# Attention of eight heads as one unrolled chain, with a one-pass causal mask and another order of the query blocks

## The chip, the cores and the metric

The kernel runs on one core of a Trainium2 chip. The metric is the device time of one execution in microseconds, as the median of several runs. A core has TensorE (PE in the profile, matmuls; its weight loads are PEld), VectorE (DVE), ScalarE (ACT), GpSimd (POOL) and SyncE (SP, which issues most transfers here). Each engine works through its own instructions in program order, and they wait for one another on semaphores.

## The reference, cut to what matters

The whole computation is a first block (modulated RMS norm, a gated short convolution, an MLP with squared ReLU) and a second block of two layers (attention and pooling, a gated feed-forward with a causal convolution, a conformer convolution, a feed-forward again), all in float32 for 512 positions of 1024 channels. The change touches the attention alone: 8 heads of 64 channels, causal, with a bias that is the difference of cumulated log forget gates.

```
q = rms_norm(q, q_g); k = rms_norm(k, k_g)            # 512 positions, 8 heads, 64 channels
c = cumsum(log_sigmoid(f_logit))                      # per position and head
s = q @ k^T * 64**-0.5 + c[query] - c[key]
s = where(key <= query, s, -inf)
out = softmax(s) @ v
```

## The kernel before, in words

Weights stream from HBM in units of 256 columns (RAW); ScalarE rounds them to WH in fp32r, VectorE keeps the rest in WL, and TensorE makes each product as three fp32r matmuls (high by high, low by high, high by low; lines 1270 to 1272). The attention stands between the input product of the even layer and its output product, and is not split into high and low: its matmuls are full f32, and each of them shows as two instructions on TensorE.

Positions are cut into 4 query blocks of 128. Query block qb needs qb + 1 key blocks. QS and KS hold two heads (97 rows: 64 channels, and rows 64 and 96 with the decay and constants, so that the score matmul of line 1442 adds the decays). A score sits negated in PSUM, hence the minimum in place of a maximum.

For a block the work goes round the engines like this. TensorE: score matmul (line 1442), then a second matmul with the identity as weights that adds MASK, an upper triangle of 1e30, to the last 128 columns (line 1443). VectorE: minimum along each row (line 1089). ScalarE: exp with the minimum as bias and the row sum as a by-product into PR (line 638). TensorE: transposes of PR's blocks (line 1451). ScalarE: copy from PSUM to PT (line 645). TensorE: value product (line 1459), two instructions for each key block. VectorE: reciprocal of the row sum (line 1092), then the scaled output into OT (line 1097).

The software pipeline is written by hand. In step s TensorE issues the score of block s, the transposes of block s-2 and the values of block s-3; ScalarE the exp of s and the copy of s-2; VectorE the minimum of s, the reciprocal of s-2, the output of s-4. Scores have four PSUM banks, the transposes two, the outputs two; PR and PT are double. The steps run over 8 blocks, those of two heads, in a hardware loop over 4 pairs of heads. Each turn of the loop fills and drains the pipeline. At its top VectorE writes QS and KS of both heads from QK (lines 1081 and 1083), ScalarE copies the decay rows from CR (lines 630 and 631), and TensorE makes three matmuls without a use, keep_busy(3, 2), which the trace has at line 1289 as six instructions. Within a head the blocks come with 1, 2, 3, 4 key blocks.

Before the loop GpSimd has begun the window sums of the pooling half (lines 411 and 417). After the loop TensorE waits for the last OT, turns OT (line 1465), makes the pooling product, and the output product follows. SyncE has loaded the first output units before.

Of the kernel before, what the change touches and what calls it, by code (L numbers as in the profile page):

```python
# [27 lines left out]
P = 128  # L28
# [86 lines left out]
ROOT_LATE = (ST_X2, ST_F0, ST_F1)  # L115


def program(nc, i, out):
    ctx = ExitStack()
    with ctx:  # L120
# [52 lines left out]
        IDENT = at("IDENT", 204.75, [P, P])  # L173
        ONES = at("ONES", 205.25, [P, P])
        BD = at("BD", 205.75, [P, P])
        MASK = at("MASK", 206.25, [P, P])
# [202 lines left out]
        def _(pool):  # L379
            for m, v in ((IDENT, 0.0), (ONES, 1.0), (BD, 0.0), (MASK, 0.0)):  # L380
                pool.memset(m[:, :], v).then_inc(s_const0, 1)
            pool.memset(sc_(S_EPS), EPS).then_inc(s_const, 1)
            pool.wait_ge(s_const0, 4)
            pool.affine_select(out=IDENT[:, :], in_=IDENT[:, :], compare_op=ALU.not_equal, fill=1.0, base=0,
                               pattern=[[-1, P]], channel_multiplier=1).then_inc(s_const, 1)

            pool.affine_select(out=MASK[:, :], in_=MASK[:, :], compare_op=ALU.is_ge, fill=MASKED, base=0,
# [34 lines left out]
            pool.memset(MASK[:, :], -1.0 / P).then_inc(g_k, 1)  # L422
# [39 lines left out]
        def _(act):  # L462
# [163 lines left out]
            with act.Fori(0, HEADS // 2) as pair:  # L626
                for h in range(2):
                    act.wait_ge(e_cr, 32)
                    act.wait_ge(a_qk, pair * 4 + (2 * h + 2))
                    act.activation(QS[64:65, h:h + 1, :], CR[64:65, ds(pair * 2 + h, 1), :], ACT.Copy).then_inc(a_row, 1)  # L630
                    act.activation(KS[96:97, h:h + 1, :], CR[96:97, ds(pair * 2 + h, 1), :], ACT.Copy).then_inc(a_row, 1)
                for s in range(10):
                    if s < 8:
                        n = (s % 4 + 1) * P
                        act.wait_ge(a_min, pair * 8 + (s + 1))
                        if s >= 2:
                            act.wait_ge(a_t, pair * 8 + (s - 1))
                        act.activation(PR[:, s % 2, 0:n], PS_[:, S_BANKS[s % 4], 0:n], ACT.Exp, scale=-1.0,
                                       bias=sc_(S_MN + s), accum_out=sc_(S_RS + s)).then_inc(a_e, 1)
                    if s >= 2:  # L640
                        k, n = s - 2, ((s - 2) % 4 + 1) * P
                        act.wait_ge(a_t, pair * 8 + (k + 1))
                        if k >= 2:
                            act.wait_ge(a_o, pair * 8 + (k - 1))
                        act.activation(PT[:, k % 2, 0:n], PS_[:, 4 + k % 2, 0:n], ACT.Copy).then_inc(a_tc, 1)
# [92 lines left out]
            for n in range(DC):  # L738
# [9 lines left out]
                for k in range(TAPS_PE[n]):  # L748
                    act.activation(DG[:, j, k, :], IDENT[:, :], ACT.Copy,
                                   scale=col("dw_w0", 8 * (TAPS - TAPS_PE[n] + k) + n)).then_inc(g_d, 1)  # L750
# [50 lines left out]
        def _(dve):  # L801
# [275 lines left out]
            with dve.Fori(0, HEADS // 2) as pair:  # L1077
                for h in range(2):
                    lo, hi = h * DH, h * DH + DH

                    stt(QS[0:DH, h:h + 1, :], QK[lo:hi, ds(pair, 1), :], small[lo:hi, S_Q8:S_Q8 + 1],
                        SQT[lo:hi, ds(pair, 1), :], ALU.mult, ALU.mult).then_inc(a_qk, 1)
                    stt(KS[0:DH, h:h + 1, :], QK[lo:hi, ds(pair + 4, 1), :], col("k_g")[lo:hi, :],
                        SQT[lo:hi, ds(pair + 4, 1), :], ALU.mult, ALU.mult).then_inc(a_qk, 1)
                for s in range(12):
                    if s < 8:
                        n = (s % 4 + 1) * P
                        dve.wait_ge(a_s, pair * 8 + (s + 1))
                        dve.tensor_reduce(sc_(S_MN + s), PS_[:, S_BANKS[s % 4], 0:n], AX.X, ALU.min).then_inc(a_min, 1)
                    if 2 <= s < 10:  # L1090
                        dve.wait_ge(a_e, pair * 8 + (s - 1))
                        dve.reciprocal(sc_(S_RR + s - 2), sc_(S_RS + s - 2)).then_inc(a_rr, 1)
                    if s >= 4:
                        k = s - 4
                        dve.wait_ge(a_o, pair * 8 + (k + 1))
                        dve.wait_ge(a_rr, pair * 8 + (k + 1))
                        dve.tensor_scalar(OT[:, k % 4, ds(pair * P + k // 4 * DH, DH)], PS_[:, k % 2, 0:DH],
                                          sc_(S_RR + k), None, ALU.mult).then_inc(a_oe, 1)
# [156 lines left out]
        def _(pe):  # L1255
# [30 lines left out]
            def keep_busy(n, bank=7):  # L1286

                for _ in range(n):
                    pe.matmul(PS_[:, bank, :], IDENT[:, :], VCOL[:, 0:T], start=True, stop=True)
# [32 lines left out]
            for t in range(VT):  # L1322
                n = TILE_ROWS[t]
                if t == 1:
                    pe.wait_ge(s_vin, 16 * (7 + 4 + 2 + 8))
                if t >= 2:
                    pe.wait_ge(s_ve, t - 1)
                pe.transpose(PS_[:, 6 + t % 2, 0:n], VROW[0:n, t, :], IDENT[0:n, 0:n]).then_inc(s_vt, 1)
                if t == 0:
                    pe.wait_ge(s_xin, 16)  # L1330
                    for c in range(DC):
                        if c >= 4:
                            pe.wait_ge(s_xe, c - 3)
                        for b in range(TB):
                            tr = pe.transpose(PS_[:, c % 4, b * P:b * P + P], XROW[:, b, c * P:c * P + P], IDENT[:, :])
                        tr.then_inc(s_xt, 1)
                    mod_product(1)
                    channel_sum(ST_X0)
# [93 lines left out]
            with pe.Fori(0, HEADS // 2) as pair:  # L1432
                keep_busy(3, 2)
                for s in range(11):
                    if s < 8:
                        h, qb, n = s // 4, s % 4, (s % 4 + 1) * P
                        pe.wait_ge(a_qk, pair * 4 + (2 * h + 2))
                        pe.wait_ge(a_row, pair * 4 + (2 * h + 2))
                        if s >= 4:
                            pe.wait_ge(a_e, pair * 8 + (s - 3))  # L1440
                        bank = PS_[:, S_BANKS[s % 4], :]
                        pe.matmul(bank[:, 0:n], QS[:, h, qb * P:qb * P + P], KS[:, h, 0:n], start=True, stop=True)  # L1442
                        pe.matmul(bank[:, n - P:n], IDENT[:, :], MASK[:, :], start=False, stop=True,
                                  skip_group_check=True).then_inc(a_s, 1)
                    if 2 <= s < 10:
                        k = s - 2
                        pe.wait_ge(a_e, pair * 8 + (k + 1))
                        if k >= 2:
                            pe.wait_ge(a_tc, pair * 8 + (k - 1))
                        for b in range(k % 4 + 1):  # L1450
                            tr = pe.transpose(PS_[:, 4 + k % 2, b * P:b * P + P], PR[:, k % 2, b * P:b * P + P], IDENT[:, :])
                        tr.then_inc(a_t, 1)
                    if s >= 3:
                        k = s - 3
                        pe.wait_ge(a_tc, pair * 8 + (k + 1))
                        if k >= 2:
                            pe.wait_ge(a_oe, pair * 8 + (k - 1))
                        for b in range(k % 4 + 1):
                            mm = pe.matmul(PS_[:, k % 2, 0:DH], PT[:, k % 2, b * P:b * P + P],  # L1459
                                           V[:, b, ds(pair * P + k // 4 * DH, DH)], start=(b == 0), stop=(b == k % 4))  # L1460
                        mm.then_inc(a_o, 1)
            pe.wait_ge(a_oe, 32)
            for c in range(4):
                for b in range(TB):
                    pe.transpose(PS_[:, c, b * P:b * P + P], OT[:, b, c * P:c * P + P], IDENT[:, :]).then_inc(a_ot, 1)
# [24 lines left out]
            def turned(nth, n):  # L1490

                for half in range(2):
                    bank = TURN_BANKS[(nth + half) % 4]
                    for b in range(2):
                        for c in range(2):
                            tr = pe.transpose(PS_[:, bank, b * UW + c * P:b * UW + c * P + P],
                                              X[:, 2 * n + c, (2 * half + b) * P:(2 * half + b) * P + P], IDENT[:, :])
                    tr.then_inc(s_yt, 1)
# [34 lines left out]
            def taps(n):  # L1533
# [12 lines left out]
                if n >= 2:  # L1546
                    mm = pe.matmul(o, MASK[:, :], CV[:, 0, :], start=False, stop=True)
# [21 lines left out]
            for n in range(DC):  # L1569
                unit_with_taps(n)  # L1570
                if n == 2:
                    pe.wait_ge(g_x, 1)
                    pe.matmul(PS_[:, TAP_BANKS[0][0], :], MASK[:, :], CV[:, 0, :], start=True, stop=True
# [64 lines left out]
```

## Time and profile before

| | |
|---|---|
| median of 3 runs | 1844.48 us (1842.78 to 2548.79) |
| profiled execution, own time | 1842.85 us |
| its span | 1841.1 us |
| busy PE / PEld / DVE / ACT / POOL | 95% / 76% / 59% / 38% / 7% |
| mean granted TensorE clock | 0.977 |
| moved by DMA | 176.14 MB, mean 96 GB/s |

The busy share of PE is that of overlapping instructions, so a start-to-start distance says more than a duration. The page also gives the chain of waits: followed back from the last instruction, at each step the thing that released it. A microsecond of work that is on that chain is a microsecond of the kernel; idle time elsewhere costs nothing.

### The profile page before, as it was taken

What the parts mean: (1) busy time and instruction counts of PE and PEld (TensorE: products, weight loads), DVE (VectorE), ACT (ScalarE), POOL (GpSimd) and SP (SyncE); (2) the same over time, 40 slices, a digit from 0 to 9 for tenths busy, and PEclk for the clock granted to TensorE, in tenths of its full rate; (3) what the DMA queues carried; (4) which work ended last, traced back from release to release, by engine and by line L of the source; (5) the groups of instructions that cost most, each with busy time, mean ns of one, the idle gap of its engine ahead of it and who ended that gap; (6) DMA issues with size and microseconds to landing.
All of it is one profiled execution on the core that took longest, in us unless ns stands there. A gap on an engine that the chain in (4) does not pass through costs nothing.

```text
span 1841.1 us, 21801 instructions
## 1 busy us (share of the span) xinstructions
PE 1754.4 (95%) x7714; PEld 1404.7 (76%) x7714; DVE 1081.0 (59%) x1647; ACT 692.5 (38%) x1000; POOL 132.3 (7%) x131
## 2 busy tenths in 40 slices
PE   4899999999999879989999999999998999999998
PEld 4788857888888658666888888877664788888887
DVE  5698846343434543545566474567998667366374
ACT  2222225231314232454443242344665454244242
POOL 0000000000000000300000000000896000000000
PEclk7799999999999989999999999999999999999999
DMA  7577412223333203200322223223221222323222
GB/s 237 161 228 229 138 46 91 92 92 94 107 96 108 69 23 115 70 1 3 106 97 92 91 91 114 91 69 92 69 69 46 69 92 91 109 81 107 91 80 80
DMA packets 182188, 176.14 MB, mean 96 GB/s; under 512 B 3160, under 2 KB 181596, under 8 KB 182124
## 3 DMA queue, kind: packets, MB, share of 16 engines
q1 hardware_dynamic: 182124, 175.29, 29.8%
q8 instruction: 39, 0.64, 0.2%
q14 instruction: 25, 0.20, 0.0%
HBM read 173.15 MB, written 2.10 MB: 95 GB/s over the span
## 4 chain that ended last, share of the span: by engine, by line
PE 89%; DVE 5%; issue 2%; ACT 2%; DMA 1%; DVEq 0%; SPq 0%; ACTq 0%
PE PSUM L1270 24%; PE PSUM L1272 24%; PE PSUM L1271 24%; PE PSUM L1544 2%; PE PSUM L1563 1%; PE PSUM L1565 1%; PE PSUM L1564 1%; PE PSUM L1315 1%; PE PSUM L1442 1%; PE PSUM L1459 1%; DMA XROW<-in_x 1%; DMA ARAW<-in_ada_w 1%; DVE SQ L821 1%; PE PSUM L1300 1%; PE PSUM L1356 0%
## 5 line engine op out<-in xcount | busy, mean ns | idle before, releaser
L472 ACT ACTIVATE WH<-RAW 128x1024 fp32r<-128x1024 f32 x280 | 287.1, 1052 | 766.9 <-PE PSUM L1272 749.4
L1270 PE MATMUL PSUM<-XH,WH 128*128 128x512 f32 x1232 | 483.1, 392 | 11.8 <-issue 10.8
L1271 PE MATMUL PSUM<-XL,WH 128*128 128x512 f32 x1232 | 480.3, 390 | 0.0
L1272 PE MATMUL PSUM<-XH,WL 128*128 128x512 f32 x1232 | 480.2, 390 | 0.0
L808 DVE TENSOR_TENSOR WL<-RAW,WH 128x1024 fp32r<-128x1024 f32 x280 | 342.3, 1246 | 10.0 <-ACT WH L472 9.4
L1270 PE MATMUL PSUM<-HH,WH 128*128 128x512 f32 x756 | 296.7, 393 | 8.1 <-DVE HL L1151 4.9
L1271 PE MATMUL PSUM<-HL,WH 128*128 128x512 f32 x756 | 295.5, 391 | 0.0
L1272 PE MATMUL PSUM<-HH,WL 128*128 128x512 f32 x756 | 295.2, 390 | 0.0
L1270 PEld LDWEIGHTS PSUM<-XH,WH 128*128 128x128 f32 x1232 | 231.9, 188 | 64.2 <-issue 15.6
L1271 PEld LDWEIGHTS PSUM<-XL,WH 128*128 128x128 f32 x1232 | 232.0, 188 | 49.0 <-issue 1.2
L1272 PEld LDWEIGHTS PSUM<-XH,WL 128*128 128x128 f32 x1232 | 231.8, 188 | 48.6
L1270 PEld LDWEIGHTS PSUM<-HH,WH 128*128 128x128 f32 x756 | 142.6, 189 | 41.1 <-DVE WL L808 5.7
L1272 PEld LDWEIGHTS PSUM<-HH,WL 128*128 128x128 f32 x756 | 142.6, 189 | 30.0
L1271 PEld LDWEIGHTS PSUM<-HL,WH 128*128 128x128 f32 x756 | 142.7, 189 | 29.5
L1127 DVE TENSOR_TENSOR ZP<-PSUM,R 128x512 f32<-128x512 f32 x88 | 56.7, 686 | 176.8 <-PE PSUM L1272 176.8
L891 DVE TENSOR_TENSOR X<-PSUM,X 128x512 f32 (+1 forms) x62 | 39.9, 685 | 158.5 <-PE PSUM L1272 152.4
L431 POOL TENSOR_TENSOR CP<-CP,PRD 128x512 f32<-128x512 f32 x68 | 93.0, 1367 | 458.8 <-ACT PRD L763 450.2
L1138 DVE SCALAR_TENSOR_TENSOR TA<-ZP,VCOL,TA 128x512 f32<-128x512 f32 x176 | 120.1, 743 | 0.0
L1203 DVE SCALAR_TENSOR_TENSOR PSUM<-UPAD,VCOL,PSUM 128x512 f32<-128x512 f32 x121 | 81.8, 747 | 0.4
L836 DVE SCALAR_TENSOR_TENSOR MACC<-ARAW,small,MACC 128x256 f32<-128x256 f32 x140 | 67.9, 485 | 5.0
L1004 DVE TENSOR_SCALAR TA<-PSUM 128x512 f32<-128x512 f32 x32 | 20.6, 685 | 84.9 <-PE PSUM L1272 84.9
L685 ACT ACTIVATE TA<-ZP,VCOL 128x512 f32<-128x512 f32 x88 | 66.7, 805 | 0.0
(237 smaller groups left out, 1671.5 us busy)
## 6 DMA issues: line engine op xcount, KB each, us to landing
RAW<-in_ffn_w_up SPq DMA_DIRECT2D x44, 1024.0 KB, 5.1
ARAW<-in_ada_w SPq DMA_DIRECT2D x24, 1024.0 KB, 5.3
RAW<-in_mlp_w_in SPq DMA_DIRECT2D x16, 1024.0 KB, 5.3
RAW<-in_mlp_w_out SPq DMA_DIRECT2D x16, 1024.0 KB, 4.9
RAW<-in_ffn_w_down SPq DMA_DIRECT2D x16, 1024.0 KB, 5.1
RAW<-in_sc_w_in SPq DMA_DIRECT2D x12, 1024.0 KB, 5.1
RAW<-in_even_w_in SPq DMA_DIRECT2D x8, 1024.0 KB, 5.4
RAW<-in_odd_w_pw SPq DMA_DIRECT2D x16, 512.0 KB, 4.7
```

The source lines that it names most:

```text
L431: pool.tensor_tensor(CP[:, n, :], CP[:, n, :], PRD[:, before % RING, :], ALU.add).then_inc(g_a, 1)
L472: act.activation(WH[:, j, a:b, :], RAW[:, j, a:b, :], ACT.Copy).then_inc(s_hi, 1)
L685: act.activation(TA[:, c, :], ZP[:, c, 2:T + 2], ACT.Identity, scale=col(f"fw{layer}2", it * 2 + (half + 2 * first + c)), bias=col(f"fb{la ...
L808: tt(WL[:, j, a:b, :], RAW[:, j, a:b, :], WH[:, j, a:b, :].bitcast(F32), ALU.subtract).then_inc(s_lo, 1)
L836: stt(dst, w, s, dst, ALU.mult, ALU.add).then_inc(s_as if k < 7 else s_ad, 1)
L891: ins = dve.tensor_copy(d, src) if first else tt(d, src, d, ALU.add)
L1127: tt(ZP[:, c, 2:T + 2], banks(j, c), R[:, :], ALU.mult).then_inc(f_z, 1)
L1138: stt(TA[:, c, :], ZP[:, c, tap:tap + T], col(f"fw{layer}{tap}", it * 2 + (half + 2 * first + c)), TA[:, c, :], ALU.mult, ALU.add).then_in ...
L1203: stt(acc, src, w, acc, ALU.mult, ALU.add).then_inc(g_v, 1)
L1270: pe.matmul(o, wh, mh[:, k, :], start=(k == 0), stop=False)
L1271: pe.matmul(o, wh, ml[:, k, :], start=False, stop=False)
L1272: mm = pe.matmul(o, wl, mh[:, k, :], start=False, stop=(k == kn - 1))
```

## The change

There is no loop over pairs any more. All 32 blocks form one chain of steps (TensorE 35, ScalarE 34, VectorE 36), written out. Head n uses half n % 2 of QS and KS. Heads 0 and 1 are prepared ahead of the chain; heads 2 to 7 inside it: VectorE's scaled_head(n) stands behind the step of the first block of head n-1, ScalarE's decay_rows(n) behind the step of its second block. keep_busy(3, 2) runs once. IDENT and MASK are declared in fp32r, so that the mask matmul is one instruction; all other uses read them as f32. The blocks of a head are taken in the order of QUERY_BLOCKS, with 4, 1, 3 and 2 key blocks.

```diff
+QUERY_BLOCKS = (3, 0, 2, 1)
-        IDENT = at("IDENT", 204.75, [P, P])
+        IDENT = at("IDENT", 204.75, [P, P], F32R)
-        MASK = at("MASK", 206.25, [P, P])
+        MASK = at("MASK", 206.25, [P, P], F32R)
...
-            with act.Fori(0, HEADS // 2) as pair:
...
+            def decay_rows(n):
+
+                act.wait_ge(e_cr, 32)
+                act.wait_ge(a_qk, 2 * n + 2)
+                act.activation(QS[64:65, n % 2, :], CR[64:65, n, :], ACT.Copy).then_inc(a_row, 1)
+                act.activation(KS[96:97, n % 2, :], CR[96:97, n, :], ACT.Copy).then_inc(a_row, 1)
+
+            decay_rows(0)
+            decay_rows(1)
+            for s in range(4 * HEADS + 2):
+                if s < 4 * HEADS:
+                    n = (QUERY_BLOCKS[s % 4] + 1) * P
+                    act.wait_ge(a_min, s + 1)
                     if s >= 2:
+                        act.wait_ge(a_t, s - 1)
+                    act.activation(PR[:, s % 2, 0:n], PS_[:, S_BANKS[s % 4], 0:n], ACT.Exp, scale=-1.0,
+                                   bias=sc_(S_MN + s % 8), accum_out=sc_(S_RS + s % 8)).then_inc(a_e, 1)
+                if s >= 2:
+                    k, n = s - 2, (QUERY_BLOCKS[(s - 2) % 4] + 1) * P
+                    act.wait_ge(a_t, k + 1)
+                    if k >= 2:
+                        act.wait_ge(a_o, k - 1)
+                    act.activation(PT[:, k % 2, 0:n], PS_[:, 4 + k % 2, 0:n], ACT.Copy).then_inc(a_tc, 1)
+                if s % 4 == 1 and 5 <= s < 4 * HEADS - 4:
+                    decay_rows(s // 4 + 1)
...
-            with dve.Fori(0, HEADS // 2) as pair:
...
+            def scaled_head(n):
+
+                lo, hi, pair = n % 2 * DH, n % 2 * DH + DH, n // 2
+                if n >= 2:
+                    dve.wait_ge(a_s, 4 * n - 4)
+                stt(QS[0:DH, n % 2, :], QK[lo:hi, pair, :], small[lo:hi, S_Q8:S_Q8 + 1], SQT[lo:hi, pair, :],
+                    ALU.mult, ALU.mult).then_inc(a_qk, 1)
+                stt(KS[0:DH, n % 2, :], QK[lo:hi, pair + 4, :], col("k_g")[lo:hi, :], SQT[lo:hi, pair + 4, :],
+                    ALU.mult, ALU.mult).then_inc(a_qk, 1)
+
+            scaled_head(0)
+            scaled_head(1)
+            for s in range(4 * HEADS + 4):
+                if s < 4 * HEADS:
+                    n = (QUERY_BLOCKS[s % 4] + 1) * P
+                    dve.wait_ge(a_s, s + 1)
...
+                if s % 4 == 0 and 4 <= s < 4 * HEADS - 4:
+                    scaled_head(s // 4 + 1)
...
-            with pe.Fori(0, HEADS // 2) as pair:
-                keep_busy(3, 2)
-                for s in range(11):
...
+            keep_busy(3, 2)
+            for s in range(4 * HEADS + 3):
+                if s < 4 * HEADS:
+                    h, qb = s // 4, QUERY_BLOCKS[s % 4]
+                    n = (qb + 1) * P
...
+                    if s >= 4:
+                        pe.wait_ge(a_e, s - 3)
+                    bank = PS_[:, S_BANKS[s % 4], :]
+                    pe.matmul(bank[:, 0:n], QS[:, h % 2, qb * P:qb * P + P], KS[:, h % 2, 0:n], start=True, stop=True)
+                    pe.matmul(bank[:, n - P:n], IDENT[:, :], MASK[:, :], start=False, stop=True,
+                              skip_group_check=True).then_inc(a_s, 1)
```

## Rows read from the trace of the kernel before

**Rows 1.** The page: shares of the chain that ended last, by engine.
```profile
PE 89%; DVE 5%; issue 2%; ACT 2%; DMA 1%; DVEq 0%; SPq 0%; ACTq 0%
```
**Rows 2.** Chain of waits in order of time, 760 to 870: start, length, what.
```profile
772.74 0.46 PE PSUM L1442 x2
...
788.45 1.12 PE PSUM L1459 x8
...
793.20 0.46 PE PSUM L1442 x2
...
828.37 3.70 PE PSUM L1289 x6
...
847.63 0.29 DVE OT L1097
...
857.33 0.23 PE PSUM L1271
```
**Rows 3.** Timeline of pair 1: start, length, engine, line, what, count, idle before.
```profile
800.73 0.86 PE L1442 MATMUL PSUM<-KS,QS 97*128 97x384 f32 x2
...
801.65 0.27 PE L1451 MATMUL PSUM<-IDENT,PR 128*128 128x128 f32 x1
...
801.76 1.00 PE L1459 MATMUL PSUM<-V,PT 128*128 x8
801.85 0.56 DVE L1089 TENSOR_REDUCE small<-PSUM 128x1 f32<-128x384 f32 x1 [1.30 <-PE PSUM L1443]
...
802.44 0.58 ACT L638 ACTIVATE PR<-PSUM,small 128x384 f32<-128x384 f32 x1 [1.02 <-DVE small L1089]
...
802.60 1.08 PE L1442 MATMUL PSUM<-KS,QS 97*128 97x512 f32 x2
...
803.51 0.39 PE L1443 MATMUL PSUM<-MASK,IDENT 128*128 128x128 f32 x2
...
803.94 0.69 DVE L1089 TENSOR_REDUCE small<-PSUM 128x1 f32<-128x512 f32 x1 [1.28 <-PE PSUM L1443]
...
804.66 0.69 ACT L638 ACTIVATE PR<-PSUM,small 128x512 f32<-128x512 f32 x1 [1.38 <-DVE small L1089]
804.80 0.15 DVE L1092 RECIPROCAL small<-small 128x1 f32<-128x1 f32 x1
...
805.34 0.75 ACT L645 ACTIVATE PT<-PSUM 128x256 f32<-128x256 f32 x2
...
805.77 0.66 PE L1459 MATMUL PSUM<-V,PT 128*128 x4 [1.15 <-ACT PT L645]
```
**Rows 4.** Groups by line and form, 789.4 to 847.5: busy, mean ns, idle before.
```profile
L1081 DVE SCALAR_TENSOR_TENSOR QS<-QK,small,SQT 64x512 f32 x6 | 4.5, 747 | 0.8 <-issue 0.7
...
L630 ACT ACTIVATE QS<-CR 1x512 f32 x6 | 3.8, 626 | 11.3 <-DVE KS L1083 11.3
...
L645 ACT ACTIVATE PT<-PSUM 128x512 f32<-128x512 f32 x6 | 3.6, 592 | 2.4 <-PE PSUM L1451 2.4
...
L645 ACT ACTIVATE PT<-PSUM 128x384 f32<-128x384 f32 x6 | 2.9, 485 | 0.0
...
L645 ACT ACTIVATE PT<-PSUM 128x256 f32<-128x256 f32 x6 | 2.2, 373 | 0.0
...
L1089 DVE TENSOR_REDUCE small<-PSUM 128x1 f32<-128x128 f32 x6 | 1.7, 291 | 4.3 <-PE PSUM L1443 4.3
```
**Rows 5.** Timeline of pair 0: its first exp.
```profile
775.56 0.37 ACT L638 ACTIVATE PR<-PSUM,small 128x128 f32<-128x128 f32 x1
```
**Rows 6.** Timeline: a scaling beside POOL's additions, and POOL's one-column operations.
```profile
769.65 1.52 DVE L1083 SCALAR_TENSOR_TENSOR KS<-QK,VCOL,SQT 64x512 f32 x1
...
779.86 7.02 POOL L417 TENSOR_SCALAR PS<-PS 128x1 f32<-128x1 f32 x26
```
**Rows 7.** Stretches: limits, length, busy (count) by engine, granted clock, DMA share, GB/s.
```profile
828.20:830.00 1.80, 1.80 (x4) 0.77 (x4) 1.24 (x3) 0.00 (x0) 0.00 (x0) 0.50 0.00 0
...
812.30:832.10 19.80, 18.19 (x99) 0.91 0.00 0
```

More of the change, by code:

```diff
@@ L380, in _ @@
             for m, v in ((IDENT, 0.0), (ONES, 1.0), (BD, 0.0), (MASK, 0.0)):
-                pool.memset(m[:, :], v).then_inc(s_const0, 1)
+                pool.memset(m[:, :].bitcast(F32), v).then_inc(s_const0, 1)
             pool.memset(sc_(S_EPS), EPS).then_inc(s_const, 1)
             pool.wait_ge(s_const0, 4)
-            pool.affine_select(out=IDENT[:, :], in_=IDENT[:, :], compare_op=ALU.not_equal, fill=1.0, base=0,
+            pool.affine_select(out=IDENT[:, :], in_=IDENT[:, :].bitcast(F32), compare_op=ALU.not_equal, fill=1.0, base=0,
                                pattern=[[-1, P]], channel_multiplier=1).then_inc(s_const, 1)
-            pool.affine_select(out=MASK[:, :], in_=MASK[:, :], compare_op=ALU.is_ge, fill=MASKED, base=0,
+            pool.affine_select(out=MASK[:, :], in_=MASK[:, :].bitcast(F32), compare_op=ALU.is_ge, fill=MASKED, base=0,
                                pattern=[[-1, P]], channel_multiplier=1).then_inc(s_const, 1)
@@ L421, in _ @@
             pool.wait_ge(a_s, 8 * (HEADS // 2))
-            pool.memset(MASK[:, :], -1.0 / P).then_inc(g_k, 1)
+            pool.memset(MASK[:, :].bitcast(F32), -1.0 / P).then_inc(g_k, 1)
             def add_scaled(n):
@@ L624, in _ @@
                         act.activation(SQT[:, n, :], SQT[:, n, :], ACT.Exp, scale=-0.5).then_inc(e_r, 1)
-            with act.Fori(0, HEADS // 2) as pair:
[L627 to L639, printed above, removed]
-                    if s >= 2:
[L641 to L645, printed above, removed]
@@ L748, in _ @@
                 for k in range(TAPS_PE[n]):
-                    act.activation(DG[:, j, k, :], IDENT[:, :], ACT.Copy,
+                    act.activation(DG[:, j, k, :], IDENT[:, :].bitcast(F32), ACT.Copy,
                                    scale=col("dw_w0", 8 * (TAPS - TAPS_PE[n] + k) + n)).then_inc(g_d, 1)
@@ L1076, in _ @@
             dve.wait_ge(e_r, 8)
-            with dve.Fori(0, HEADS // 2) as pair:
[L1078 to L1098, printed above, removed]
@@ new lines, in _ @@
+            scaled_head(0)
[4 more added lines that the diff above has]
+                    dve.wait_ge(a_s, s + 1)
+                    dve.tensor_reduce(sc_(S_MN + s % 8), PS_[:, S_BANKS[s % 4], 0:n], AX.X, ALU.min).then_inc(a_min, 1)
+                if 2 <= s < 4 * HEADS + 2:
+                    dve.wait_ge(a_e, s - 1)
+                    dve.reciprocal(sc_(S_RR + (s - 2) % 8), sc_(S_RS + (s - 2) % 8)).then_inc(a_rr, 1)
+                if s >= 4:
+                    k = s - 4
+                    dve.wait_ge(a_o, k + 1)
+                    dve.wait_ge(a_rr, k + 1)
+                    dve.tensor_scalar(OT[:, QUERY_BLOCKS[k % 4], k // 4 * DH:k // 4 * DH + DH], PS_[:, k % 2, 0:DH],
+                                      sc_(S_RR + k % 8), None, ALU.mult).then_inc(a_oe, 1)
+                if s % 4 == 0 and 4 <= s < 4 * HEADS - 4:
+                    scaled_head(s // 4 + 1)
@@ L1288, in keep_busy @@
                 for _ in range(n):
-                    pe.matmul(PS_[:, bank, :], IDENT[:, :], VCOL[:, 0:T], start=True, stop=True)
+                    pe.matmul(PS_[:, bank, :], IDENT[:, :].bitcast(F32), VCOL[:, 0:T], start=True, stop=True)
             def channel_sum(stat):
@@ L1327, in _ @@
                     pe.wait_ge(s_ve, t - 1)
-                pe.transpose(PS_[:, 6 + t % 2, 0:n], VROW[0:n, t, :], IDENT[0:n, 0:n]).then_inc(s_vt, 1)
+                pe.transpose(PS_[:, 6 + t % 2, 0:n], VROW[0:n, t, :], IDENT[0:n, 0:n].bitcast(F32)).then_inc(s_vt, 1)
                 if t == 0:
@@ L1334, in _ @@
                         for b in range(TB):
-                            tr = pe.transpose(PS_[:, c % 4, b * P:b * P + P], XROW[:, b, c * P:c * P + P], IDENT[:, :])
+                            tr = pe.transpose(PS_[:, c % 4, b * P:b * P + P], XROW[:, b, c * P:c * P + P], IDENT[:, :].bitcast(F32))
                         tr.then_inc(s_xt, 1)
@@ L1431, in _ @@
             pe.wait_ge(s_ev, U_EVEN + 8)
-            with pe.Fori(0, HEADS // 2) as pair:
-                keep_busy(3, 2)
-                for s in range(11):
[L1435 to L1461, printed above, removed]
@@ new lines, in _ @@
+            keep_busy(3, 2)
[3 more added lines that the diff above has]
+                    n = (qb + 1) * P
+                    pe.wait_ge(a_qk, 2 * h + 2)
+                    pe.wait_ge(a_row, 2 * h + 2)
+                    if s >= 4:
+                        pe.wait_ge(a_e, s - 3)
[3 more added lines that the diff above has]
+                              skip_group_check=True).then_inc(a_s, 1)
+                if 2 <= s < 4 * HEADS + 2:
+                    k = s - 2
+                    pe.wait_ge(a_e, k + 1)
+                    if k >= 2:
+                        pe.wait_ge(a_tc, k - 1)
+                    for b in range(QUERY_BLOCKS[k % 4] + 1):
+                        tr = pe.transpose(PS_[:, 4 + k % 2, b * P:b * P + P], PR[:, k % 2, b * P:b * P + P], IDENT[:, :].bitcast(F32))
+                    tr.then_inc(a_t, 1)
+                if s >= 3:
+                    k = s - 3
+                    pe.wait_ge(a_tc, k + 1)
+                    if k >= 2:
+                        pe.wait_ge(a_oe, k - 1)
+                    for b in range(QUERY_BLOCKS[k % 4] + 1):
+                        mm = pe.matmul(PS_[:, k % 2, 0:DH], PT[:, k % 2, b * P:b * P + P],
+                                       V[:, b, k // 4 * DH:k // 4 * DH + DH], start=(b == 0), stop=(b == QUERY_BLOCKS[k % 4]))
+                    mm.then_inc(a_o, 1)
@@ L1464, in _ @@
                 for b in range(TB):
-                    pe.transpose(PS_[:, c, b * P:b * P + P], OT[:, b, c * P:c * P + P], IDENT[:, :]).then_inc(a_ot, 1)
+                    pe.transpose(PS_[:, c, b * P:b * P + P], OT[:, b, c * P:c * P + P], IDENT[:, :].bitcast(F32)).then_inc(a_ot, 1)
             pe.wait_ge(s_wp, 16)
@@ L1496, in turned @@
                             tr = pe.transpose(PS_[:, bank, b * UW + c * P:b * UW + c * P + P],
-                                              X[:, 2 * n + c, (2 * half + b) * P:(2 * half + b) * P + P], IDENT[:, :])
+                                              X[:, 2 * n + c, (2 * half + b) * P:(2 * half + b) * P + P], IDENT[:, :].bitcast(F32))
                     tr.then_inc(s_yt, 1)
@@ L1546, in taps @@
                 if n >= 2:
-                    mm = pe.matmul(o, MASK[:, :], CV[:, 0, :], start=False, stop=True)
+                    mm = pe.matmul(o, MASK[:, :].bitcast(F32), CV[:, 0, :], start=False, stop=True)
                 mm.then_inc(g_m, 1)
@@ L1572, in _ @@
                     pe.wait_ge(g_x, 1)
-                    pe.matmul(PS_[:, TAP_BANKS[0][0], :], MASK[:, :], CV[:, 0, :], start=True, stop=True
+                    pe.matmul(PS_[:, TAP_BANKS[0][0], :], MASK[:, :].bitcast(F32), CV[:, 0, :], start=True, stop=True
                               ).then_inc(g_n, 1)
```

## The prediction

> **What bounds the kernel now.** I read the page's chain of waits first: TensorE carries 89% of it [rows 1]. So a change pays only where TensorE waits on that chain. The edit touches one such stretch, the attention. The chain in order of time shows it from the first score matmul of the stage (772.74, pair 0; the same row of pair 1 is at 793.20) to the last scaled output, an OT row at 847.63 [rows 2]: 75 us. Inside it there are three pauses between pairs. The last value product of pair 0 begins its eight passes at 788.45 and has finished at 789.57, and pair 1's first score starts at 793.20: 3.63 us. The pause after pair 1 repeats this to 0.01 us, the third is the row of 3.70 us with keep-busy matmuls. Together 11.0 us, in which VectorE scales the next two heads and ScalarE copies their decay rows, while PE multiplies for nothing.
>
> Next I read the timeline of pair 1 for the rhythm of a step [rows 3]. Two passes of 512 score columns take 0.91 us (802.60 to 803.51), a transpose 0.11, eight value passes 0.84 (801.76 to 802.60), so 0.105 each. A head has 10 score blocks, 4 masks, 10 transposes and 20 value passes. With masks at 0.11 that is 2.28 + 0.44 + 1.10 + 2.10 = about 5.9 us of PE work a head, 47 us for eight: the floor of the stage.
>
> **The links that can't be packed.** In step s PE issues score and mask of block s, transposes of s-2, values of s-3. VectorE takes the minimum of s, ScalarE exponentiates s and only then copies the transposes of s-2; the values of s-2 wait for that copy, and score s+2 stands behind them on PE. So from one score to the score two steps later there is a link: score and mask, minimum, exp, copy of s-2, values of s-2. With 4, 1, 3, 2 the four- and three-block steps fall on the same parity, so a head's heavy links follow one another, and the light parity (1 and 2) runs in their shadow.
>
> **The mask.** Today it is two passes at full f32; the VectorE minimum starts 0.43 after the first of them (803.51 to 803.94) [rows 3]. One pass goes: 0.11. An fp32r matmul of 128 columns isn't in the trace. The nearest is one of 512 columns, which holds the chain for 0.23 us [rows 2], half of an f32 pass's 0.455; by columns that gives 0.06 for 128. Its own end can so come 0 to 0.05 earlier. I take 0.14 off each link, with 0.11 and 0.16 as ends; a loss is excluded only as long as the same weight load isn't slower in fp32r, and the rows of rows 2 show none that is. Over 15 links: 2.1 us (1.7 to 2.4).
>
> **Link A, four blocks to three.** Score to minimum, 802.60 to 803.94, 1.34, less 0.14 = 1.20. Minimum to exp 0.72 (803.94 to 804.66), exp to copy 0.68 (804.66 to 805.34) [rows 3]. Copy of three blocks 0.49 [rows 4], 0.05 to PE (the two-block copy starts at 805.34 and is 0.37 long [rows 4], the values that wait for it start at 805.77 [rows 3]), six value passes 0.63. Sum 3.77.
> **Link B, three to four.** Score to minimum 800.73 to 801.85, 1.12, less 0.14 = 0.98; minimum to exp 0.59 (801.85 to 802.44) [rows 3]; exp 0.57; copy of four blocks 0.59 [rows 4]; 0.05; eight value passes 0.84. Sum 3.62.
> A head so takes 7.39, against 5.9 of PE work: 1.5 of stall stays.
>
> **The moved head work.** scaled_head(n) now stands on VectorE behind the four-block step, decay_rows(n) on ScalarE behind the one-block step, six times each. Behind the scaled head waits the minimum of the one-block step, then its exp, the copy of s-1, the decay rows, and behind those the exp of the three-block step. From the four-block score: 1.20 to the minimum; 0.86 until VectorE is through with minimum, reciprocal and output (803.94 to 804.80) [rows 3]; two scalings, which follow each other at about 0.67 to 0.75 [rows 4], 1.40; one-block minimum 0.29 [rows 4] and 0.04 on; exp 0.34 (its row is 0.37 long, the accumulator read starts before its end) [rows 5]; copy 0.27; two row copies of 0.63 and a start each [rows 4], 1.30. Sum 5.70. The three-block exp would be due at 3.77 + 0.98 + 0.59 = 5.34. It comes about 0.35 late, so a head with inserts takes 7.7; the rest of 2.7 us a head is hidden by the links. What hides it is the long link A; with a shorter one it would show.
>
> **Start and end.** The first exp is held by the second head's rows, which come before the loop in both kernels, so it stays at 775.56 [rows 5], now of four blocks: its accumulator is read at 0.78, four transposes and hand-over 0.65, the exp of step 2 0.57, copy of step 0 0.59, values 0.89: the score of head 1 at 779.1. Six periods of 7.7 lead to head 7's at 825.3. Link A, link B (no inserts): 832.7. Then on PE three transposes, a one-block value product and two transposes while the copy of three blocks is made: values of it at 833.7, then those of the last block, and the last OT at about 835.0 in place of 847.63. **Sum: 12.6 us less.** Everything behind it, the OT transposes first, waits for the last OT and moves along. SP's loads of the output weights are issued before the pairs begin and stay where they are. The register updates of the loops go too; they lie inside the links already counted or in the pauses. keep_busy stays once, not four times; it stood in the pauses.
>
> The profiled execution took 1842.85 us; less 12.6 gives 1830.3. The median of the three runs is 1.6 higher, which gives 1831.9. I say 1831.
>
> **A cost that the trace doesn't decide.** The first inserted scaling (near 781) meets POOL's 26 one-column operations, which last from 779.86 for 7.02 us; a scaling beside POOL's full-width additions took 1.52 instead of 0.75 [rows 6]. Beside one-column ones none ran. Ends: 0, and doubled, 1.5 us later once. I take 0, since these are far smaller than the additions. The Trainium skill (GPSIMD Engine Reference, Specifications) says that GpSimd shares its SBUF interfaces with VectorE and contends with instructions of two SBUF inputs, which a scaling is; by it the sum would lie up to 1.5 lower in gain, at 11.1.
>
> **Rivals.**
> *The inserts show in full.* If the three-block exp or minimum really queues behind them, 2.3 of the 2.7 us more appear in each of six heads: 14 us, and the gain is gone: 1844. For it: both queues are in order. Against: the timing above, which leaves them about 2.3 us of shadow.
> *TensorE becomes the bound.* If the latencies of the two parities overlap better than I chain them, six periods shrink from 7.7 to 5.9 and the stalls of both ends by about 1: 12 us more, 1819. For it: in the middle of pair 1 PE runs from 798.5 to 804.4 with no stall; its last steps are in [rows 3]. Against: that was the order 1, 2, 3, 4, in which the heavy blocks alternate with light ones on each parity. By my own links the old order in one chain would be quicker (its 2 and 4 chain gives about 6.6 a head); the order, taken alone, costs.
> *The clock falls: the slower side.* The place is the stall of 1.2 us in link A and 0.9 in link B, in every head, with the keep-busy matmuls gone. Once before the clock did fall in this stage: the granted clock was 0.50 between 828.20 and 830.00, behind the end of pair 2, where TensorE stands idle for about 1.15 us (the same place of pair 1 shows it, the idle time before the value product at 805.77) [rows 3, 7]. At 1.2 GHz a head is 11.8 us of PE work. All heads so: 94 us and 3 to 4 for the ends, some 22 longer than before: 1866. It decides from the point at which a head averages 9.4 (75 over 8), that is when over two fifths of the heads run at 1.2 GHz. A single fall remains within my case: that pair with its pause took 19.8 us at a mean of 0.91, and 0.09 of 19.8 is 1.8 us of clock lost at most, part of it in the pause. The Trainium skill (TensorE: Matmul & The Clock Gate, A second HAM failure mode) describes kernels in which short idles between groups of matmuls make the clock swing between its levels; here the rows show one fall in four pairs, so it happens, but not as a rule.
> *The change does not do what it says:* the mask still runs as two passes. Then 1.7 to 2.4 us are missing: 1833.
>
> **Chances.** My sum, with a stray clock fall or two, 0.68; inserts in full or most of it 0.10; PE as the bound 0.09; mask not halved 0.04; clock low enough to be slower than before 0.09. The time is the first one's: 1831. Its own spread: 0.4 us a period gives 3 either way, contention 1.5, clock falls up to 4: 1826 to 1838. To leave out only 2 in 10 the range takes in half of the way to the PE-bound case and most of the way to the case of visible inserts: 1823 to 1841. Two per cent of the kernel, about what a measurement can tell from no change, is 37 us. The stage would have to shrink to 38 us, under its 47 of PE work, or grow by half; faster 0.01, slower 0.02, within 0.97.
>
> **What would show it.** Right: no rows of keep-busy matmuls after 772; the mask as one instruction a block, 32 in all, where it is two now [rows 3]; four-block scores 7.7 us apart, the last OT near 835; the exp of the three-block step waiting for nothing on VectorE but for ScalarE's own row copies; PE idle twice a head, before the values of three and of four blocks, until the copy. Wrong: periods under 6.5 (PE bound), minimum rows of the one-block step that delay the three-block ones (inserts), a granted clock under 0.9 over the stage, or a scaling of 1.5 us at 781.

## The result, and the profile after

The changed kernel takes 1835.85 us in the median of 8 runs (1832.73 to 1838.79), the kernel before 1843.77; the ratio is 0.9946, 95% interval 0.9931 to 0.9962. One of the 8 runs of the kernel before took 2548.79 us; it hardly moves the median, and the ratio leaves it out. In a later series it was 1832.67 against 1844.35, ratio 0.9935 (0.9918 to 0.9952). The forecast was 1831, within 1823 to 1841, a gain of 12.6; measured were 7.9 us in the first series and 11.7 in the later one. The profiled execution took 1836.98 us, its span is 1835.2.

The page's shares of the chain of waits, as in [rows 1]:

```profile
PE 88%; DVE 5%; ACT 3%; issue 2%; DMA 1%; DVEq 0%; SPq 0%; ACTq 0%
```

The timeline of after (start, length, engine, line, operation, count, idle time before): the first score of the stage, then one head from its four-block score to the next head's.

```profile
777.62 1.10 PE L1454 MATMUL PSUM<-KS,QS 97*128 97x512 f32 x2 [1.93 <-DVE QS L1088]
...
784.19 1.08 PE L1454 MATMUL PSUM<-KS,QS 97*128 97x512 f32 x2
...
784.70 0.63 PE L1455 MATMUL PSUM<-MASK,IDENT 128*128 128x128 f32 x1
784.82 7.23 POOL L418 TENSOR_SCALAR PS<-PS 128x1 f32<-128x1 f32 x24
...
785.37 0.69 DVE L1099 TENSOR_REDUCE small<-PSUM 128x1 f32<-128x512 f32 x1 [2.40 <-PE PSUM L1455]
...
786.09 0.69 ACT L642 ACTIVATE PR<-PSUM,small 128x512 f32<-128x512 f32 x1 [2.28 <-DVE small L1099]
...
786.23 0.73 DVE L1088 SCALAR_TENSOR_TENSOR QS<-QK,small,SQT 64x512 f32<-64x512 f32 x1
...
787.30 0.88 PE L1471 MATMUL PSUM<-V,PT 128*128 128x64 f32 x6 [0.89 <-ACT PT L649]
...
788.02 0.86 PE L1454 MATMUL PSUM<-KS,QS 97*128 97x384 f32 x2
...
791.12 1.10 PE L1471 MATMUL PSUM<-V,PT 128*128 128x64 f32 x8 [0.68 <-ACT PT L649]
...
792.07 1.08 PE L1454 MATMUL PSUM<-KS,QS 97*128 97x512 f32 x2
```

The mask is one instruction now. TensorE waits twice in the head, 0.89 us before the values of three blocks and 0.68 before those of four, each time for the copy (line 649). These are the two links of the prediction: 3.83 us from the four-block to the three-block score, 4.05 back.

The chain of waits of after in order of time (start, length, what) over the same head, and the last OT row:

```profile
784.35 0.91 PE PSUM L1454 x2
...
786.24 0.72 DVE QS L1088
786.96 0.66 DVE KS L1090
787.62 0.21 DVE small L1099
...
788.31 0.27 ACT PT L649
...
788.61 0.63 ACT QS L631
...
789.91 0.58 ACT PR L642 x2
790.49 0.59 ACT PT L649
...
791.12 1.10 PE PSUM L1471 x8
792.23 0.91 PE PSUM L1454 x2
...
841.86 0.30 DVE OT L1107
```

In [rows 2] the pauses between pairs stood here. Now the way round a head leads over the scaled head on VectorE (lines 1088, 1090), the one-block minimum and exp, a copy, the decay rows on ScalarE (631), and only then the three-block exp. The stage lasts from 777.62 to 841.86, 64.2 us in place of 74.9: 10.7 us less. But it begins 4.9 us later than in the trace of before, and what follows the last OT is as long as before (993.3 us against 993.5). So 5.9 us of the profiled execution's time are gained, not 10.7. The 4.9 us lie upstream, in code that the change leaves alone. One place shows in the granted clock. These are the same stretches of before and of after (limits, length, PE busy and count, granted clock, DMA share, GB/s):

```profile
210.00:240.00 30.00, 30.00 (x152) 0.89 0.26 81
...
680.00:720.00 40.00, 30.41 (x151) 0.83 0.30 86
```
```profile
210.00:240.00 30.00, 30.00 (x142) 0.80 0.31 98
...
680.00:720.00 40.00, 29.24 (x130) 0.83 0.27 79
```

0.09 of 30 us is 2.7 us, more than half of the 4.9; where the rest arose stays open. In all twelve later profiles the stage begins between 772.4 and 775.2, so 777.6 is the latest start seen, of code that the change leaves alone.

### The profile page after: what moved, and what is told of

The parts are those of the page before. It is cut to its first block, busy times and chain, and to the rows that moved or that the text cites. A ratio compares the mean times of both kernels' runs of the same rounds, so it can differ in the third digit from the quotient of the medians.

```text
span 1835.2 us, 21490 instructions
## 1 busy us (share of the span) xinstructions
PE 1742.8 (95%) x7664; PEld 1398.7 (76%) x7664; DVE 1079.3 (59%) x1647; ACT 691.6 (38%) x1000; POOL 133.1 (7%) x131
## 4 chain that ended last, share of the span: by engine, by line
PE 88%; DVE 5%; ACT 3%; issue 2%; DMA 1%; DVEq 0%; SPq 0%; ACTq 0%
PE PSUM L1282 24%; PE PSUM L1283 24%; PE PSUM L1284 24%; PE PSUM L1556 2%; PE PSUM L1575 1%; PE PSUM L1577 1%; PE PSUM L1576 1%; PE PSUM L1327 1%; DMA XROW<-in_x 1%; PE PSUM L1471 1%; PE PSUM L1368 1%; DMA ARAW<-in_ada_w 1%; DVE SQ L827 1%; PE PSUM L1312 1%; PE PSUM L1614 0%
## 5 line engine op out<-in xcount | busy, mean ns | idle before, releaser
L1282 PE MATMUL PSUM<-XH,WH 128*128 128x512 f32 x1232 | 483.6, 393 | 11.8 <-issue 10.8
L1282 PEld LDWEIGHTS PSUM<-XH,WH 128*128 128x128 f32 x1232 | 232.1, 188 | 64.4 <-issue 15.6
```

The costliest lines, as they stand in the source:

```text
L1282: pe.matmul(o, wh, mh[:, k, :], start=(k == 0), stop=False)
```

## The experiments

Below, "stage" is the time from the start of the first score row to the start of the last OT row, "period" the time from one four-block score to the next. The first four experiments are single executions on one chip, on which the kernel before took 1845.47 us; they are read by the stage and the period, not by the time. "The best version" is the changed kernel with the copy first and the decay rows early. No run takes the loop over pairs away and leaves mask and order as they were.

**The order alone undone.**
```diff
-QUERY_BLOCKS = (3, 0, 2, 1)
+QUERY_BLOCKS = (0, 1, 2, 3)
```


> The chain of after with the query blocks of a head in the order 1, 2, 3, 4 again; all else of the change stays. The stage (first score row to last OT row) took 64.2 us in after, 74.9 before. Link theory (mine): the heavy links then join 2 and 4 blocks, by the rows 3.25 + 3.49 = 6.7 us a head without inserts, some 7.3 with the scaled head in front of the two-block minimum; the stage shrinks to 60 to 61 us. Rival (the order 4, 1, 3, 2 is what fills the stalls): the stage grows to 66 us or more.

Stage 67.4 us, time 1837.1 (one run). By that number the rival won. The chain of waits and the clock say otherwise. First the four-block scores in order of time, then two stretches:

```profile
778.38 1.71 PE PSUM L1454 x2
...
789.57 1.81 PE PSUM L1454 x2
...
800.87 1.81 PE PSUM L1454 x2
...
808.86 0.91 PE PSUM L1454 x2
...
815.68 0.91 PE PSUM L1454 x2
...
822.50 0.91 PE PSUM L1454 x2
```
```profile
778.00:802.00 24.00, 24.00 (x88) 0.50 0.00 1
...
804.00:806.00 2.00, 2.00 (x13) 0.71 0.00 0
```

From 778 to about 805 the clock stood at half, 1.2 GHz, and TensorE was busy without a gap (24.00 of 24.00 us); a head took 11.2 to 11.3 us. At full clock the period is 6.8 us, against 7.9 to 8.0 in after. The order 4, 1, 3, 2, in this chain, costs 1.1 us a head at full clock, as my links said, a little more than I had thought. The three slow periods (11.2, 11.3 and 8.0 in place of 6.8) cost 10 us. Without them the stage would be 57; that is worked out, not run.

**The mask as two passes again, in the chain.**
```diff
-                    pe.matmul(bank[:, n - P:n], IDENT[:, :], MASK[:, :], start=False, stop=True,
+                    pe.matmul(bank[:, n - P:n], IDENT[:, :].bitcast(F32), MASK[:, :].bitcast(F32), start=False, stop=True,
```


> After with the mask matmul read as f32 again, so two instructions a block. Link theory: one more pass of 0.11 us and a later end, 0.11 to 0.16 us on each of 15 heavy links, the stage 1.7 to 2.4 us longer, 66 to 66.6. Rival (the mask lies beside other work, because TensorE stalls anyway): 64.2, no change.

Stage 67.6, time 1836.52 (one run), again with a fall of the clock, here to 0.57 on average from 780 to 788. At full clock the chain has these four-block scores, five periods apart:

```profile
790.89 0.91 PE PSUM L1454 x2
...
831.51 0.91 PE PSUM L1454 x2
```

Two periods, a longer and a shorter one, take 8.11 on average, 0.17 more than in after. The mask pass is on the path, but by this number once a head (I had 0.14 for each) and not twice: the path round a head goes through the four-block mask and then over the inserts, past the three-block mask. So the mask is worth 0.17 x 7 or some 1.2 us of the stage, not 2.1.

**The decay rows earlier.**
```diff
-                act.wait_ge(a_qk, 2 * n + 2)
+                if n >= 2:
+                    act.wait_ge(a_s, 4 * n - 4)
+                else:
+                    act.wait_ge(a_qk, 2 * n + 2)
...
+                if s % 4 == 0 and 4 <= s < 4 * HEADS - 4:
+                    decay_rows(s // 4 + 1)
...
-                if s % 4 == 1 and 5 <= s < 4 * HEADS - 4:
-                    decay_rows(s // 4 + 1)
```


> After with decay_rows(n) moved from behind the one-block step to ahead of the exp of the four-block step, with a wait for the scores of head n-2 in place of the wait for the scaled head. ScalarE is idle there for 2.3 us. My account: the row copies make the three-block exp 0.3 to 0.5 us late in six heads; they go, the period falls from 7.95 to about 7.5, the stage to 61.5 to 62.5. Rival (the scaled head on VectorE, through the late one-block minimum and exp, is what is late): 64.2 or less than 0.5 us below.

The rows now wait for the scores of head n-2, the last to read that half of QS and KS. Stage 67.4, time 1837.49 (one run), with the clock at half from 781 to 798. Four-block scores on the chain at full clock:

```profile
810.09 0.91 PE PSUM L1457 x2
...
817.63 0.91 PE PSUM L1457 x2
...
825.17 0.91 PE PSUM L1457 x2
```

7.54 us, as expected; the rows behind the one-block step had cost 0.4 a head. The stage's total missed the expectation by the fall.

**The copy ahead of the exp.** ScalarE's two operations of a step exchanged. The copy's inputs are ready by then anyway: the exp already waited for the transposes of s-2, as it overwrites their PR.
```diff
+                if s >= 2:
+                    k, n = s - 2, (QUERY_BLOCKS[(s - 2) % 4] + 1) * P
+                    act.wait_ge(a_t, k + 1)
...
+                    act.activation(PT[:, k % 2, 0:n], PS_[:, 4 + k % 2, 0:n], ACT.Copy).then_inc(a_tc, 1)
                 if s < 4 * HEADS:
...
                     act.activation(PR[:, s % 2, 0:n], PS_[:, S_BANKS[s % 4], 0:n], ACT.Exp, scale=-1.0,
...
-                if s >= 2:
-                    k, n = s - 2, (QUERY_BLOCKS[(s - 2) % 4] + 1) * P
...
```


> After with ScalarE's two operations of a step exchanged: the copy of block s-2 ahead of the exp of block s. Link theory: the copy is made while VectorE takes the minimum, so minimum and exp of s leave the path to the values of s-2; no heavy link is left and TensorE's own work of about 5.9 us a head is the bound: period 6.0 to 6.5, the stage 52 to 55 us. Rival (the stall lies in the hand-overs or in VectorE, not in the place of the copy): the stage stays within 2 us of 64.2.

Stage 57.1, time 1825.71 (one run), the stage at full clock throughout, period 7.1. That lies between the two expectations: the link broke, but one wait remained. The timeline:

```profile
804.89 0.63 ACT L631 ACTIVATE QS<-CR 1x512 f32<-1x512 f32 x1
...
805.54 0.63 ACT L632 ACTIVATE KS<-CR 1x512 f32<-1x512 f32 x1
...
806.19 0.60 ACT L642 ACTIVATE PT<-PSUM 128x512 f32<-128x512 f32 x1
...
806.84 1.10 PE L1471 MATMUL PSUM<-V,PT 128*128 128x64 f32 x8 [0.65 <-ACT PT L642]
```

The copy of four blocks starts as the decay rows end. So the next run has both edits.

**Copy first and decay rows early**, the two edits above (the decay rows stand ahead of the copy of the four-block step).

> The copy ahead of the exp and the decay rows ahead of the copy of the four-block step. In the run with the copy first alone the period was 7.1 us, because the copy of four blocks queued behind the decay rows. Link theory: with those gone TensorE is the bound: 5.95 us of its work a head and about 0.3 of weight loads after waits, period 6.1 to 6.4, the stage 51 to 53 us at full clock, some 12 us under after. Rival (ScalarE's or VectorE's own work is the bound): period stays at 7.1, the stage at 57.

Median 1820.02 us, ratio to before 0.9863 (0.9847 to 0.9880). The stage is 51.4 us. The four-block scores in the timeline:

```profile
797.35 1.08 PE L1457 MATMUL PSUM<-KS,QS 97*128 97x512 f32 x2
803.61 1.08 PE L1457 MATMUL PSUM<-KS,QS 97*128 97x512 f32 x2
809.66 1.08 PE L1457 MATMUL PSUM<-KS,QS 97*128 97x512 f32 x2
```

6.05 and 6.26 by turns, 6.16 on average, with PE busy 7.96 of 8 us:

```profile
796.00:804.00 8.00, 7.96 (x56) 1.00 0.01 2
```

TensorE is the bound, as the 5.9 us of its work a head said; 0.26 a head is left over. The stage is 12.8 us shorter than after's, but behind the last OT this profiled run took 996.6 us and not 993.3, with a fall of the clock near 1785 that after's does not have; a shorter stage need not come through in full. The median is 15.8 us under after's first series, which is another series and so no fair comparison; the same-chip one follows below.

**The same with the order 1, 2, 3, 4.**

> As the run before, with the query blocks in the order 1, 2, 3, 4. If no latency link is left, the order does not matter: the same period within 0.15 us. Rival (some link stays): the orders differ by over 0.3 us a head.

Median 1833.43, ratio 0.9940 (0.9924 to 0.9957), stage 58.6 with a fall of the clock between 776 and 783. At full clock the period is 6.98, so the rival is right, by 0.8 us a head. Over seven periods that is under 6 us, but on the same chip the medians lie 13.4 us apart. The profiled run, with 1830.24 the fastest of the four, lost about 3.4 us to its fall; the other three have lower mean clocks (0.970 to 0.972, against 0.976 to 0.977 without the change of order). So with this order the clock seems to have cost as much again as the links; where it fell in the three is not shown. The timeline gives the reason for the 0.8:

```profile
803.04 0.63 ACT L635 ACTIVATE KS<-CR 1x512 f32<-1x512 f32 x1
...
803.69 0.49 ACT L647 ACTIVATE PT<-PSUM 128x384 f32<-128x384 f32 x1
...
804.23 0.88 PE L1474 MATMUL PSUM<-V,PT 128*128 128x64 f32 x6 [0.67 <-ACT PT L647]
```

With one key block in the first step ScalarE has no long idle stretch before the copy, so the inserted rows delay it. The order 4, 1, 3, 2 gives the inserts a shelter; whether it helps depends on what else bounds the head. It lost 1.1 us a head with the exp first, and won 0.8 with the copy first and the rows early.

**Useless matmuls at the start of the chain**, in the best version and in the changed kernel itself.
```diff
-            keep_busy(3, 2)
+            keep_busy(5, 2)
...
+                if s == 2:
+                    keep_busy(2, 0)
```


> Copy first, decay rows early, order 4, 1, 3, 2, and useless matmuls in the two idle stretches at the start of the chain: five in place of three before the first score, two before the first transposes. Clock theory: the thin start is what lets the granted clock fall (it fell there in three of five profiles), so with it filled the clock stays at 1.00 over the stage and the runs scatter less than those of the run without. Rival (falls come at random): the clock falls as often, times within 1 us of the run without.

> The changed kernel itself with the same useless matmuls at the start of the chain, nothing else. Clock theory: no fall in the stage, 64.2 us in the profile; the median moves from 1835.9 to the lower end of after's runs, 1832 to 1833.5, with a spread of 3 us in place of 6. Rival (falls at random, or the spread is from elsewhere): median 1835 to 1837 and the same spread.

Medians 1823.19 and 1832.71; in both profiles the clock is 1.00 all through the stage (51.5 and 64.4 us). The first is 3 us slower in the median than without, on the same chip; the stages differ by 0.1, and the cause stays open. The second looked like a gain of 3 over after's first series. So that both stand in one series, they were run together:

> The changed kernel again, beside the next three on one chip. Clock theory: times in groups, 1832 to 1833 where the clock holds in the stage and 1835 to 1839 where it falls, a median of 1835 to 1837, and a profile whose stage is 64.2 us or, with a fall in its first 10 us, 66 to 68. Rival (the spread has another source): no link between a time and the granted clock of its run.

> The changed kernel with useless matmuls in the two idle stretches at the start of the chain. Clock theory: on the same chip 2 to 4 us under the run without them in the median, most times at 1832 to 1833. Rival (falls at random, the median of 1832.7 in the earlier series was luck): within 1 us of the run without them, with the same spread.

After 1832.67 (1832.31 to 1836.37), with the fillers 1833.45 (1832.72 to 1836.65): the rival's answer, no gain in time. After's median also missed its expectation of 1835 to 1837, but its times do come in groups that go with the clock: four of after's six runs at 1832.3 to 1832.8 with a mean clock of 0.978, two at 1835.4 and 1836.4 with 0.976. In profiles of chain kernels without fillers the clock fell at the start of the stage in five of nine (the four runs with other orders, masks or row places, and the best version below), in after itself in none of two, with fillers in none of three. That the fillers prevent a fall is suggested by this and not shown.

**The best version again, and the mask alone.**

> Copy ahead of the exp, decay rows ahead of the copy, the order 4, 1, 3, 2. The stage was 51.4 us and the median 1820.0 on another chip. Link theory: 12.5 to 16 us under the changed kernel on the same chip. Rival (part of that was the chip's): under 10.

1821.92 us, 10.8 under the changed kernel on that chip, ratio to before 0.9866 (0.9845 to 0.9887): between the two expectations. Its profile has a fall, 0.50 from 778 to 788, and a stage of 56.0 in place of 51.4. So the best version isn't spared the falls.

> The kernel before with nothing but the mask in one pass, the loop over pairs kept. Link theory: the middle of a pair is bound by TensorE, so a pass of 0.11 us counts there on most of the 8 blocks, at the ends of a pair on the latency instead: 0.6 to 0.9 us a pair, the stage 71.4 to 72.6 in place of 74.9, the time 2.4 to 3.5 us less. Rival (the mask pass runs beside the minimum's wait and costs nothing in pairs): 74.5 or more.

```diff
-        IDENT = at("IDENT", 204.75, [P, P])
+        IDENT = at("IDENT", 204.75, [P, P], F32R)
-        MASK = at("MASK", 206.25, [P, P])
+        MASK = at("MASK", 206.25, [P, P], F32R)
```
(all else as before, the other uses read as f32.) 1851.85 us, 1850.15 to 1854.17 in nine runs, ratio 1.0037 (1.0025 to 1.0049): less work on TensorE and a slower kernel. Neither theory had this. The chain, first scores of the third and fourth pair, and one stretch:

```profile
818.93 0.46 PE PSUM L1442 x2
...
837.26 0.46 PE PSUM L1442 x2
```
```profile
778.00:798.00 20.00, 19.52 (x75) 0.50 0.00 1
```

A pair at full clock takes 18.3 us. Before, pair 1 took 19.1: it starts at 793.20 [rows 2], the next pair at 812.31. The 0.8 saved is what the link theory expected. But the clock was at half from 776 to 800, and the stage is 79.5 us, 4.6 longer. It fell once more from 851 to 858, just behind the stage, and what follows the last OT took 995.8 us in place of 993.5. All nine runs have a mean clock of 0.968 to 0.970, where the kernel before has 0.973 to 0.977, so the falls seem to come in each of them; that is inferred from their means, as only one was profiled. Nor does a run show that the missing pass is what brings them on.

## Why the prediction was right

The measured median lies inside the stated range in both series. Of the 12.6 us the stage gave 10.7.

**The pauses and the chain of waits:** right. All three pauses are gone, and no keep-busy rows stand in the stage.

**Links and inserts, term by term.** From the four-block score to the three-block exp I had 5.70 us; in after it is 784.19 to 789.91, 5.72, over the queue that I named (scaled head, one-block minimum and exp, copy, row copies). That it agrees to 0.02 is partly luck. The timeline of after:

```profile
787.55 0.27 DVE L1099 TENSOR_REDUCE small<-PSUM 128x1 f32<-128x128 f32 x1
...
788.21 0.37 ACT L649 ACTIVATE PT<-PSUM 128x256 f32<-128x256 f32 x1
...
788.61 0.63 ACT L631 ACTIVATE QS<-CR 1x512 f32<-1x512 f32 x1
```

I had called the copy behind the one-block exp that of s-1 and put it at 0.27. It is the copy of s-2, two blocks, and takes 0.40 from its start to the row copy (788.21 to 788.61): 0.13 too little. Against that the two scalings took 1.32 (786.23 to 787.55) and not 1.40, and minimum and hand-overs were some 0.03 shorter. In every other head the way is 0.13 longer, since the scaled head starts that much later. From there the copy starts at 0.57 and PE at 1.21, as summed. The values of four blocks then take 0.95 to the next score, not 0.84. This is the mis-sized term that nothing offset: I took the spacing of value passes from [rows 3] where they follow other work, but behind a wait the first of them has its weight load still to do (the weight load of the values starts with them, at 791.12; of those at 785.50, with no wait, it starts at 785.39). The row of 805.77 there, four passes after a wait, could have told. It is 0.11 a period, and again in the start and the end of the chain. The rest of the period's 0.25 is 0.07 for the longer way in every other head, 0.02 for the 5.72, and 0.05 that I lost by rounding a sum of 7.74 or 7.75 to 7.7. The run with the rows early gives the two parts apart: 7.54 for the links without the rows in the way, where I had 7.39, and 0.41 for the lateness, where I had 0.35. Period 7.95 in place of 7.7, start 6.6 in place of 6.35, end 10.0 in place of 9.7: 64.2 us against my 62.3. That is the 1.9 us between 12.6 and 10.7. In the start the way from the first exp to that of step 2 also took 1.59 us (780.45 to 782.04) and not 1.43.

**The mask:** about 1.2 us and not 2.1, since a head's path passes one mask of the two. My period with inserts already contained this; only the separate sum over 15 links was wrong.

**The order:** I had said that it costs when taken alone, and it does, 1.1 us a head at full clock (by my links 0.8: 7.4 against 6.6). I had not seen that the other order could cost clock: both chains with it fell to half (for 27 and 7 us), against three of the seven without fillers in the order 4, 1, 3, 2. So few profiles don't show a link.

**POOL beside VectorE:** the scaling at 786.23 took 0.73 us amid POOL's one-column operations (784.82, 24 of them in 7.23 us), so zero was the right end. What the Trainium skill (GPSIMD Engine Reference, Specifications) says of shared SBUF interfaces agrees with the 1.52 us beside additions [rows 6]; beside the one-column operations this trace shows no cost.

**The rivals.** Inserts in full: no, 0.4 us late a head by the run with the rows early. TensorE as the bound: not in this kernel; it took the copy first and the rows early to get there. Mask unchanged: no, one instruction. **The clock** was the rival with the most in it. In after's two profiles the stage runs at 1.00 throughout, but small edits of the same chain fell to half clock for 7 to 27 us, at its start and not at the stalls of its links as I had placed it. I held the mask to be safe; alone in the loop it saved its 0.8 us a pair, and the kernel was slower all the same, with the clock at half for 24 us. That the fall, and not another cost, made the loss is what the profile shows; that the mask made the fall is not shown.

Beyond that, the first series gave 7.9 and not the stage's 10.7. In its profiled run the missing time was not in the attention: 4.9 us lie ahead of it. The other seven have no trace. Six of the eight have a mean clock of 0.973 to 0.976 and take 1835.4 us or more, the two with 0.978 take 1832.7 and 1833.0; so the time goes with the clock, but where it fell in them is not shown. The later series, in whose profile the stage starts at 773.0 and lasts 64.2 again, gives 11.7. That its difference of medians is 1.0 above the stage's gain, and so nearer to the forecast, comes from outside the stage and is no credit to the sum. So part of the nearness of 1831 to 1832.67 is luck.

## What to carry to other kernels

In a pipeline written by hand, write down for each engine's queue which operation stands ahead of which, and sum the loop from one step to the step that it releases; here the forecast period came out 3% short (7.7 for 7.95). Then ask which of the two operations of an engine's step has its inputs first: exchanging them took 7.1 us off the stage, and 12.8 with the decay rows moved too, where the whole change took 10.7. Judge an edit of half a per cent by its stage at full clock and by the granted clock of each run, since a fall at another place can be as large as the edit.

## What the runs showed of the hardware

In these runs a TensorE at 1.2 GHz that was busy without a pause did not always come back at once: it stayed there for some 27 us in the run with the order undone (24.00 busy of 24.00 us, granted 0.50), 24 us in the one with the mask alone (19.52 busy of 20.00) and 17 us in the one with the decay rows early, but only some 7 us in the order 1, 2, 3, 4 with the copy first. These are f32 matmuls and transposes of 64 to 512 columns. What ends such a stretch stays open.

With one f32 pass of 128 columns taken out of each block of the looped kernel, all nine runs were slower than the median before, 1850.15 us or more against 1844.35. Why its start should be thinner than that of the kernel before by enough to matter, I cannot say from the traces.

One fp32r matmul of 128 columns in place of two f32 passes brought the minimum forward by 0.16 us, at the far end of what I had given (0.11 to 0.16) and 0.02 over the 0.14 that I took: from the four-block score to the minimum 1.18 us in after, 1.34 before [rows 3].
